# Wider gate weights and an earlier norm root in the opening of a two-block transformer kernel

## The reference

```
xn   = rmsnorm(h, a_norm)
proj = xn @ w_in                       # q, k, v, z: 8 heads of 128 each; b, a: 8 + 8 gate columns
qkv  = silu(causal_conv4(proj[q, k, v]))
q, k = l2norm(q) * 128 ** -0.5, l2norm(k)
beta = sigmoid(b)
g    = -exp(A_log) * softplus(a + dt_bias)
o    = chunk_gated_delta_rule(q, k, v, beta, g)
```

## Time and profile before

| | us |
|---|---|
| median of 3 runs | 1966.76 |
| lowest, highest | 1966.6, 1968.76 |
| profiled execution | 1973.58 |
| its span | 1971.6 |
| PE busy | 1893.5 |
| DVE busy | 1189.0 |
| ACT busy | 797.0 |
| POOL busy | 27.0 |

### The profile page before, as it was taken

One profiled execution on the slowest core, in us unless ns is written; L12 is line 12 of the kernel. 1 busy time (PEld: TensorE's weight loads), 2 busy tenths in 40 slices (PEclk: granted clock), 3 DMA queues, 4 the chain that ended last, 5 costly groups with the idle time before them and its releaser, 6 DMA issues.

```text
span 1971.6 us, 25290 instructions
## 1 busy us (share of the span) xinstructions
PE 1893.5 (96%) x8816; PEld 1503.6 (76%) x8816; DVE 1189.0 (60%) x1804; ACT 797.0 (40%) x1256; POOL 27.0 (1%) x51
## 2 busy tenths in 40 slices
PE   7999999879999999999999999999999999899997
PEld 4788888757888888877777778888887766677875
DVE  6777777745776763356655567776434565565444
ACT  5444444424444442244444444444333444453222
POOL 0000000000000000000000000000000000000000
PEclk9999999889999999999999999999999999999999
DMA  5411121102222232122212122222321301123221
GB/s 188 134 57 60 56 61 32 65 22 92 92 94 96 96 109 96 62 96 73 76 53 75 65 96 96 92 89 88 127 73 48 102 21 65 59 75 104 88 85 65
DMA packets 42958, 158.75 MB, mean 81 GB/s; under 512 B 5232, under 2 KB 5488, under 8 KB 42912
## 3 DMA queue, kind: packets, MB, share of 16 engines
q1 hardware_dynamic: 38304, 143.77, 21.6%
q0 software_dynamic: 4032, 14.26, 2.6%
q10 hardware_dynamic: 576, 0.11, 0.0%
HBM read 155.69 MB, written 6.63 MB: 82 GB/s over the span
## 4 chain that ended last, share of the span: by engine, by line
PE 89%; DVE 6%; ACT 3%; issue 2%; DMA 0%; DVEq 0%; ACTq 0%
PE acc L484 21%; PE acc L486 21%; PE acc L485 21%; PE acc L508 8%; PE pb L618 2%; PE pc L633 2%; PE pa L780 2%; PE pd L801 1%; ACT wsplit L964 1%; DVE wsplit L1407 1%; PE pd L622 1%; PE pc L853 1%; PE pa L599 1%; PE pa L583 1%; PE pa L839 1%
## 5 line engine op out<-in xcount | busy, mean ns | idle before, releaser
L484 PE MATMUL acc<-xhi,wsplit 128*128 128x512 f32 x1200 | 499.2, 416 | 8.4 <-DVE wsplit L1407 7.4
L486 PE MATMUL acc<-xhi,wsplit 128*128 128x512 f32 x1200 | 476.4, 397 | 0.0
L485 PE MATMUL acc<-xlo,wsplit 128*128 128x512 f32 x1200 | 476.2, 397 | 0.0
L964 ACT ACTIVATE wsplit<-wraw 128x1024 fp32r<-128x1024 f32 (+1 forms) x252 | 275.1, 1096 | 451.7 <-PE acc L486 418.1
L1407 DVE TENSOR_TENSOR wsplit<-wraw,wsplit 128x1024 fp32r<-128x1024 f32 (+1 forms) x252 | 319.9, 1273 | 158.3 <-ACT wsplit L964 156.1
L484 PEld LDWEIGHTS acc<-xhi,wsplit 128*128 128x128 f32 x1200 | 226.7, 189 | 70.8 <-issue 12.9
L485 PEld LDWEIGHTS acc<-xlo,wsplit 128*128 128x128 f32 x1200 | 227.1, 189 | 58.8 <-issue 4.8
L486 PEld LDWEIGHTS acc<-xhi,wsplit 128*128 128x128 f32 x1200 | 226.4, 189 | 55.1
L508 PE MATMUL acc<-xhi,wsplit 128*128 128x512 f32 x464 | 159.3, 412 | 0.0
L484 PE MATMUL acc<-hid_hi,wsplit 128*128 128x512 f32 x352 | 139.5, 396 | 0.0
L485 PE MATMUL acc<-hid_lo,wsplit 128*128 128x512 f32 x352 | 139.5, 396 | 0.0
(11 more groups left out here) (315 smaller groups left out, 2743.8 us busy)
## 6 DMA issues: line engine op xcount, KB each, us to landing
wraw<-w SPq DMA_DIRECT2D x220, 512.0 KB, 3.3
wraw<-w SPq DMA_DIRECT2D x32, 704.0 KB, 4.0
bias_dram<-ext_dram POOLq DMA_DIRECT2D x1, 4096.0 KB, 20.5
bias<-bias_dram POOLq DMA_DIRECT2D x8, 512.0 KB, 4.0
h<-xT SPq DMA_DIRECT2D x4, 512.0 KB, 7.1
crow<-row_dram POOLq DMA_DIRECT2D x8, 256.0 KB, 3.8
brow<-row_dram POOLq DMA_DIRECT2D x8, 256.0 KB, 4.4
outT<-h SPq DMA_DIRECT2D x8, 256.0 KB, 2.2
```

What stands on the lines that cost most here:

```text
L484: mm(out, whi[:, k, :], a[:, x_at + k, :], start=(k == first), stop=False)
L485: mm(out, whi[:, k, :], b[:, x_at + k, :], start=False, stop=False)
L486: m = mm(out, wlo[:, k, :], a[:, x_at + k, :], start=False, stop=(k == last))
L964: A(split(s, j, 0), raw(s, j), ACT.Copy).then_inc(w_hi_ready, 1)
```

## The change

What it does, engine by engine:

- `wg_hi` and `wg_lo` become 128 columns wide, of which 16 hold weights. GpSimd clears them first (two memsets), and they lie where `gd`, `tn` and `tt` are later. The gate matmuls write all 128 partitions of the bank.
- The gains' load goes from ACT's queue to the head of SP's.
- On ACT the square of slice 0 comes before the cast of `wg_hi`. The cast of tile (-1, 3) comes before the root, its low part on DVE before the gates. ACT's first gate exponential comes before q's newest tap.
- On DVE q's three older taps are spread between the gate steps; `take` of k and `low` of (0, 0) come after `rows` and `nbe`. PE does the running sums and the turns at other points of tiles (-1, 2) and (-1, 3).
- On ACT one table load now stands before `silu` of q (as before) and one right behind `square_qk`. `silu` of v, with a third table load ahead of it, comes behind the roots of q and k, `decay` and `ecrow_of`. PE turns k and v separately.
- `cast` and `low` of (0, 1) and of (0, 2) move behind the roots and behind `first_tn`.

The core of the diff:

```diff
-        wg_hi = r.sb("wg_hi", [P, KD, 16], F32R)
-        wg_lo = r.sb("wg_lo", [P, KD, 16], F32R)
+        r = Region(gates_at)
+        wg_hi = r.sb("wg_hi", [P, KD, P], F32R)
+        wg_lo = r.sb("wg_lo", [P, KD, P], F32R)
 # SP
+                    sp.dma_start(vec[:, 0:V_ACONV], vecs[:, 0:V_ACONV]).then_inc(ev("gains_landed"), 16)
                     load_x(0)
 # GpSimd
+            nc.gpsimd.memset(wg_hi[:].bitcast(F32), 0.0).then_inc(ev("wg_zeroed"), 1)
+            nc.gpsimd.memset(wg_lo[:].bitcast(F32), 0.0).then_inc(ev("wg_zeroed"), 1)
             pool.dma_start(relf[:], rel_flip).then_inc(ev("rel_landed"), 16)
 # TensorE
-                    mm(acc[0:16, 2, :], wg_hi[:, k, :], xhi[:, k, :], start=(k == 0), stop=False)
+                    mm(acc[:, 2, :], wg_hi[:, k, :], xhi[:, k, :], start=(k == 0), stop=False)
...
-            tile(s, -1, 2, k0=3)
-            tile(s, -1, 3, k1=2)
+            tile(s, -1, 2, k0=3, k1=6)
             pe.wait_ge(ev("gate_dve"), at(GATE_DVE, "gg_ready"))
...
-            tile(s, -1, 3, k0=2, k1=4)
+            tile(s, -1, 2, k0=6)
             pe.wait_ge(ev("gate_dve"), at(GATE_DVE, "cc_ready"))
...
-            tile(s, -1, 3, k0=4)
+            tile(s, -1, 3)
...
-            strips(s, 0, (0, 1), 0, 3 * KD + 6)
+            strips(s, 0, (0, 1), 0, 3 * KD)
...
-            turns(0)
+            turn_k(0)
             gram(0)
-            strips(s, 0, (0, 1), 3 * KD + 6, 2 * 3 * KD - 8)
+            strips(s, 0, (0, 1), 3 * KD, 3 * KD + 6)
+            turn_v(0)
+            strips(s, 0, (0, 1), 3 * KD + 6, 2 * 3 * KD - 10)
             first_turn(0)
-            strips(s, 0, (0, 1), 2 * 3 * KD - 8, 2 * 3 * KD)
+            strips(s, 0, (0, 1), 2 * 3 * KD - 10, 2 * 3 * KD)
 # ACT
-            act.dma_start(vec[:, 0:V_ACONV], vecs[:, 0:V_ACONV]).then_inc(ev("gains_landed"), 16)
             act.dma_start(wg[:], w_gates).then_inc(ev("wg_landed"), 16)
...
                 A(normed(k), h[:, k, :], ACT.Square).then_inc(ev("h_squared"), 1)
+                if k == 0:
+                    act.wait_ge(ev("wg_landed"), 16)
+                    act.wait_ge(ev("wg_zeroed"), 1)
+                    A(wg_hi[:, :, 0:16], wg[:], ACT.Copy).then_inc(ev("wg_hi_ready"), 1)
...
             cast(s, -1, 2)
+            act.wait_ge(acc_done, 1)
+            cast(s, -1, 3)
             root(0)
...
-            conv_newest(2, 0, -1)
             tables("silu_and_others")
             silu(-1, 1)
+            act.wait_ge(acc_done, 2)
+            cast(s, 0, 0)
+            conv_newest(2, 0, -1)
             silu(-1, 2)
             square_qk(-1)
-            act.wait_ge(acc_done, 3)
+            tables("natural_log_exp_and_others")
             conv_newest(3, 0, -1)
-            cast(s, 0, 1)
-            silu(-1, 3)
...
-            tables("natural_log_exp_and_others")
             qk_norms(0)
+            act.wait_ge(acc_done, 3)
+            cast(s, 0, 1)
             decay(0)
+            ecrow_of(0)
+            tables("silu_and_others")
+            silu(-1, 3)
             cast_ahead(s, 0, 0, False)
             kend_of(0)
             bv_of(0)
-            ecrow_of(0)
 # DVE
             low(s, -1, 2)
+            low(s, -1, 3)
...
             take(-1, 1)
-            low(s, -1, 3)
...
+            conv_older(-1, 1, 0, (1,))
             dve.wait_ge(ev("gate_act"), at(GATE_ACT, "gate_ln"))
...
-            take(-1, 2)
-            low(s, 0, 0)
+            conv_older(-1, 1, 0, (3,))
...
             stt(nbe[:], nbe[:], -1.0, beta[:], ALU.mult, ALU.mult).then_inc(ev("gate_dve"), 1)
+            take(-1, 2)
+            low(s, 0, 0)
             conv_older(-1, 2, 0)
...
             conv_older(-1, 3, 0)
-            low(s, 0, 1)
...
             exponent(0)
+            low(s, 0, 1)
             take(0, 0)
-            low(s, 0, 2)
             gram(0)
             first_tn(0)
+            low(s, 0, 2)
```

More of the change, by code:

```diff
@@ L186, in build @@
         dec = r.sb("dec", [P, NC, P])
+        gates_at = r.at
         gd = r.sb("gd", [P, NC, 2, P])
@@ L536, in _ @@
                         pe.wait_ge(ev("wg_lo_ready"), 1)
-                    mm(acc[0:16, 2, :], wg_hi[:, k, :], xhi[:, k, :], start=(k == 0), stop=False)
-                    mm(acc[0:16, 2, :], wg_hi[:, k, :], xlo[:, k, :], start=False, stop=False)
-                    m = mm(acc[0:16, 2, :], wg_lo[:, k, :], xhi[:, k, :], start=False, stop=(k == KD - 1))
+                    mm(acc[:, 2, :], wg_hi[:, k, :], xhi[:, k, :], start=(k == 0), stop=False)
+                    mm(acc[:, 2, :], wg_hi[:, k, :], xlo[:, k, :], start=False, stop=False)
+                    m = mm(acc[:, 2, :], wg_lo[:, k, :], xhi[:, k, :], start=False, stop=(k == KD - 1))
                     if k == KD - 1:
@@ L585, in sums_of, with turn_k @@
                     m.then_inc(ev("qk_sums"), 1)
-            def turns(i):
+            def turn_k(i):
                 pe.wait_ge(ev("kn_ready"), i + 1)
@@ L591, in turns, with turn_v @@
                 m.then_inc(ev("k_turned"), 1)
+            def turn_v(i):
+                pe.wait_ge(ev("qkv_silu"), i * 3 + 3)
                 for t in range(NC):
@@ L685, in delta @@
                 if not last:
-                    turns(i + 1)
+                    turn_k(i + 1)
+                    turn_v(i + 1)
                     gram(i + 1)
@@ L1057, in _ @@
             A(t0[:], gates[:, 0:8, :], ACT.Exp, scale=-1.0).then_inc(ev("gate_act"), 1)
+            act.wait_ge(ev("consts_landed"), 32)
+            conv_newest(1, 0, -1)
             act.wait_ge(ev("gate_dve"), at(GATE_DVE, "gate_abs"))
@@ L1442, in _ @@
                     dve.wait_ge(ev("wg_hi_ready"), 1)
-                    tt_(wg_lo[:], wg[:], wg_hi[:].bitcast(F32), ALU.subtract).then_inc(ev("wg_lo_ready"), 1)
+                    dve.wait_ge(ev("wg_zeroed"), 2)
+                    tt_(wg_lo[:, :, 0:16], wg[:], wg_hi[:, :, 0:16].bitcast(F32), ALU.subtract).then_inc(ev("wg_lo_ready"), 1)
                 dve.wait_ge(ev("h_squared"), k + 1)
@@ L1458, in take, with conv_older @@
                 tt_(out, acc[:, j % 2, :], rstd[:], ALU.mult).then_inc(acc_free, 1)
+            def conv_older(i, j, head, taps=(1, 2, 3)):
+                w = vec[:, V_ACONV + 32 * (j - 1):V_ACONV + 32 * j].rearrange("p (h t) -> p h t", t=4)
+                if 1 in taps:
+                    dve.wait_ge(ev("conv_newest"), i * 3 + (3 + j))
+                for d in taps:
+                    if d > 1:
+                        dve.wait_ge(ev("conv_tap"), i * 6 + (6 + 2 * (j - 1) + d - 1))
+                    x = stt(ys[:, j - 1, d:S], tmp[:, j % 2, 0:S - d], w[:, head, 3 - d:4 - d], ys[:, j - 1, d:S],
+                            ALU.mult, ALU.add)
+                    x.then_inc(ev("conv_tap") if d < 3 else ev("conv_done"), 1)
             dve.wait_ge(ev("rstd_ready"), 1)
@@ L1480, in _ @@
             stt(gg[:], gg[:], -1.0, alog[:].unsqueeze(2).to_broadcast(hc), ALU.mult, ALU.mult).then_inc(ev("gate_dve"), 1)
-            def conv_older(i, j, head, taps=(1, 2, 3)):
-                w = vec[:, V_ACONV + 32 * (j - 1):V_ACONV + 32 * j].rearrange("p (h t) -> p h t", t=4)
-                if 1 in taps:
-                    dve.wait_ge(ev("conv_newest"), i * 3 + (3 + j))
-                for d in taps:
-                    if d > 1:
-                        dve.wait_ge(ev("conv_tap"), i * 6 + (6 + 2 * (j - 1) + d - 1))
-                    x = stt(ys[:, j - 1, d:S], tmp[:, j % 2, 0:S - d], w[:, head, 3 - d:4 - d], ys[:, j - 1, d:S],
-                            ALU.mult, ALU.add)
-                    x.then_inc(ev("conv_tap") if d < 3 else ev("conv_done"), 1)
-            dve.wait_ge(ev("consts_landed"), 32)
-            conv_older(-1, 1, 0)
+            conv_older(-1, 1, 0, (2,))
             flat = lambda t: t[:].rearrange("p h t -> p (h t)")
```

10 lines of the change are left out of this document (1 added, 9 removed).

## The result

| | before | changed |
|---|---|---|
| median, us | 1967.48 (6 runs) | 1975.63 (6 runs) |
| lowest, highest | 1966.6, 1968.76 | 1971.92, 1977.4 |
| profiled execution | 1973.58 | 1977.4 |
| its span | 1971.6 | 1975.4 |
| mean granted clock | 0.986 | 0.989 |

The ratio is 1.0038, with a 95% interval from 1.0025 to 1.0051. The forecast was 1962.9 us, in a range that ended at 1966.0, and 0.05 for slower: the change is slower, by a mechanism that none of the rivals named.

The account below looks back on a forecast made before the run. TensorE, busy 96% of the span, was taken as the bound, so only its waits or low clock could yield. Gains of 0.7 + 0.3 + 1.2 + 1.7 = 3.9 us took 1966.8 to 1962.9 us, range 1960.0 to 1966.0.

Parts of the forecast that it names:

- X: Mark where the first level of head 0 starts, 59.78 us before; forecast at 55.9.
- if waits behind X grow: Sign of being wrong: TensorE's waits become longer after the first level of head 0 starts.
- rival D: Whole kernel: slower through new clock falls behind short waits, about 1.7 us each; 1967.1 to 1968.8 us, chance 0.05.
- Opening, up to T: From kernel start to the first projection tile's end: earlier gate weights and x slices move it by -0.7 us.
- T: Mark where the first projection tile is finished and the norm's sum starts, 24.92 us before; forecast 24.0 to 24.4.
- The gains' cost to x: SP's queue in the opening: the gains' issue ahead delays x's first part by 0.4 us, landing at 6.0.
- the moment of the clock's rise: Opening, 39 matmuls after TensorE's restart: the 0.9 us earlier restart is worth 0.5 to 0.9, by when the clock rises.
- From T to the squares: From the first projection tile's end to TensorE's sums for q and k: sums start at T + 15.35, -0.3 us.
- `tt`: From the sums to the first level: `tt` ready 0.9 us ahead of TensorE, so its wait goes, -1.2 us.
- The clock at the sums: TensorE's sums for q and k: a 1.8 us wait is short enough that the clock stays up, -1.7 us.
- rival A: The clock falls at the sums as before; gain only 2.2 us, time 1964.6, chance 0.23.
- rival B: Opening: the clock rises before the restart at 12.9, T at 22.1, time 1960.8 us, chance 0.18.

Follow-up runs that it names:

- the second experiment: The kernel before, with one load of the silu tables on ACT right ahead of the loop over the heads; 1976.38 against 1970.87 us, ratio 1.0028.
- narrow gates: The changed kernel with ln and exp loaded at the loop's entry, gate weights 16 columns wide again without memsets; 1966.83 against 1970.87 us, ratio 0.9978.
- silu at the round's end: The changed kernel with each round's silu table load moved from its middle to its end, behind o_hi; 1967.73 against 1969.22 us, ratio 0.9992.
- ln at entry: Same kernel as the first experiment: the changed kernel plus an ln and exp table load before the loop; 1968.16 against 1970.87 us, ratio 0.9981.
- gains on ACT: The changed kernel with ln and exp at the loop's entry, gains' load back at the head of ACT's queue; 1966.11 against 1970.87 us, ratio 0.9973.
- two idle loads: The changed kernel with ln and exp at the loop's entry, plus two unneeded table loads ending each round; 1968.36 against 1971.21 us, ratio 0.9984.
- v's silu first: The changed kernel with v's silu ahead of the roots again and no third table load before the loop; 1968.79 against 1969.22 us, ratio 1.0002.
- the first experiment: The changed kernel with one more load of the ln and exp tables on ACT right before the loop; 1968.16 against 1970.87 us, ratio 0.9981.

## Why the prediction was wrong, point by point

**The step that failed** is in its first paragraph: "The diff touches the code ahead of the loop over the heads and nothing behind it", and from it "From X on, everything follows from what stands before it, so the time changes by what X moves". X moved by -0.72 in the profiled execution and the time by +8.15 in the medians. What the opening hands to the loop is more than a time: it is also the set of tables that is active on ACT, and the diff changed it, by the third `tables` of the opening. The price is in the rows: 6 rounds of 1.28 us, 7.7 us. The prediction did name "if waits behind X grow" as a sign of being wrong, and that is the sign that came, 7.3 us of it. It could have been seen without a run. The diff shows which set each path brings to `conv_newest`; what its source does not show is the load itself, since nobody wrote it. The Trainium skill (ScalarE: Activation LUTs, section "Step-by-step: what each stage is for") says that a load is placed ahead of an activation whose set is not active. The trace agrees and goes further: the activation at L1053 is only a scaled copy, and it got a load in every round. For the price, the section "What ACT_TABLE_LOAD costs" of that page of the Trainium skill adds a drain of some 1.38 us to the load's 1.28; in the row of 109.23 above the copy starts 1.30 behind the load's start, and it is the same where the load directly follows an activation, in the changed kernel at the sums. So the trace shows the load alone.

```profile
40.56 0.61 ACT L1063 ACTIVATE sq<-ys 128x512 f32<-128x512 f32 x1
41.19 1.28 ACT L1085 ACT_TABLE_LOAD   x1
42.49 0.72 ACT L1053 ACTIVATE ys<-tmp,vec 128x512 f32<-128x512 f32 x1
```

**Slower** was given 0.05, all of it to rival D, new falls of the clock. D did not happen: the clock granted over the execution was 0.989, for 0.986 before. The "new wait" was looked for in the opening only.

**Opening, up to T: -0.7 forecast, +0.77 in the profiled execution.** The terms were of two kinds. The gains' cost to x, 0.4, was near: the first slice starts 0.5 later with the gains on SP's queue, by the medians of the executions above. But in the profiled execution of the changed kernel x itself came later:

```profile
1.34 6.13 DMA h<-xT
```

It landed at 7.47, 1.5 later than forecast, so TensorE restarted at 14.36 instead of 12.9. `wg` took 2.2 us instead of 4.9 to 6.4 and nobody waited for it. The other kind was the moment of the clock's rise. The forecast bounded what 39 matmuls gain by it, and T was 25.69 with the rise at 18.57, while T lies near 22.5 where the clock was up at the restart, in the old order too (22.88 in the second experiment). That term is larger than the whole of the rest, and no run shows it to be the change's. Where the clock was up at the restart in either order the two can be compared: T is 22.14 to 22.55 in the new order (five executions) and 22.88 and 22.99 in the old one, 0.3 to 0.9 earlier, and the forecast of 0.7 lies in that.

**From T to the squares: -0.3 forecast, -0.11 measured.** By its steps: `gg` complete at T + 5.64 (forecast 5.6), `rows` copied at T + 8.05 (8.1), k's taps at T + 11.32 (11.2), the sums at T + 15.54 (15.35). This part of the working held to 0.2 us. The wait was 1.9 for 1.8.

**`tt`: -1.2 forecast, confirmed.** The wait is gone in the changed kernel. `kn` starts 4.9 behind the sums' start (4.3 forecast, with the sums at the low clock), v's silu ends at 51.95 and nobody waits for it. The experiment with v's silu ahead of the roots puts a number to it: without this move three waits of 0.5 return.

**The clock at the sums: -1.7 forecast, not in the profiled execution.** It fell behind a wait of 1.9 us: rival A, given 0.23. With the same wait it stayed up in others. This is the time from the turned gates to X in each profiled execution with that wait, X from the chain (the last kernel has v's silu back in its old place):

| kernel | gates turned to X, us | wait at the sums | clock at the sums |
|---|---|---|---|
| before | 31.84 | 2.2 | fell |
| silu at entry, old order | 31.83 | 2.2 | fell |
| changed | 30.28 | 1.9 | fell |
| narrow gates | 30.36 | 1.9 | fell |
| silu at the round's end | 30.31 | 1.9 | fell |
| ln at entry | 28.69 | 1.9 | stayed |
| gains on ACT | 28.68 | 1.9 | stayed |
| two idle loads | 28.68 | 1.9 | stayed |
| v's silu first | 30.98 | 1.9 | stayed |

So behind the turned gates the change's order is worth 1.55 us where the clock falls (forecast 0.3 + 1.2), and 1.6 more where it stays (forecast 1.7). The size was right; that it would be kept each time was not. The forecast reasoned from the length of the wait, 1.8 us against 2.07 and 2.17. Of seven executions with a wait of 1.9 us three lost the high clock and four kept it, so the length of this wait did not decide; seven are too few to name a chance.

**The sum.** Three kernels have the change without the loads in the loop: ln and exp at the entry (0.9981, 0.9972 to 0.999), silu at the round's end (0.9992, 0.9984 to 1.0001) and two idle loads (0.9984, 0.9974 to 0.9994). By the middles the change is then worth 3.7, 1.6 and 3.2 us of 1970, where the forecast summed up 3.9. So the opening gains something. 3.9 is above all three middles, inside the intervals of the first and the third, and beyond that of the second (3.2 at most). Where it comes near it is partly luck, as two terms of the sum were right by halves. The loop's six loads take 7.7 us by the trace, at least twice what the opening brings. From the first experiment to the changed kernel it is 11 us by the middles of the ratios; the 7.7 lies inside what their intervals leave (from 6.9), and the rest is not explained.

Two terms of the working don't add up as written: 12.9 and 9.0 make 21.9 and not rival B's 22.1, and the parts given for `kn` make 4.1 and not 4.3. Neither bears on the result.

**What stays open.** Why x landed 1.5 us later in one execution was not settled. In the six other profiled executions with the same order of loads it took 4.6 to 5.0 us and not 6.1, so the order alone doesn't make it. What sets the moment at which the clock rises in the opening stays open too.

## What to carry to other kernels

A change ahead of a loop also changes the state in which the loop is entered: go through each engine's state (on ACT the active set of tables) at the entry and at the end of a round, and make them the same before counting anything else. In the profile, compare the number of instructions of each engine first: seven more on ACT, where the source has one more, named the cause in one row. And before moving a matmul, or a wait, ask whether the engine that TensorE waits for next has slack; where it hasn't, the time filled in one place comes back in the next.

## What the runs showed of the hardware

- A table load takes 1283 ns in every group of every trace here, whichever set. Where the next activation waits for nothing else it starts 1.29 to 1.35 us after the load's start.
- Loads at the head of a queue are not of one price: `wg`, 64 KB, landed in 2.2 us as first on ACT's queue and the gains, 32 KB, in 2.0 to 2.1 us as first on SP's, ahead of x, in all seven profiled executions with this order. With the gains first on ACT's queue and x first on SP's the gains took 4.8 to 5.1 us and `wg` 5.8 to 6.4 in all six (4.9 and 6.4 before). Why was not tested.

```profile
wg<-w_gates ACTq DMA_DIRECT2D x1, 64.0 KB, 2.2
...
vec<-vecs SPq DMA_DIRECT2D x1, 32.0 KB, 2.0
```

- A memset of 128x1024 on GpSimd took 0.95 us, where 1.05 was worked out from one of 64x512.
- The same wait of 1.9 us was followed by a fall of the granted clock to 0.50 in three executions, and the clock stayed at 1.00 in four. The runs of one kernel spread over some 3 to 7 us (before: 1966.5 to 1973.5). In the stretch of the same matmuls above, two executions differ by 3.2 us, the shorter at the higher granted clock.
